# Delta rule of twelve heads on one Trainium2 core: inverse in 64x64 blocks, products by row halves, last norm by token

## The reference

```python
def rwkv7_scan(r, w, k, v, kk, a):
    def step(state, inp):
        r_t, w_t, k_t, v_t, kk_t, a_t = inp
        sa = jnp.einsum('bhvk,bhk->bhv', state, -kk_t)
        state = (state * w_t[:, :, None, :]
                 + sa[..., None] * (kk_t * a_t)[:, :, None, :]
                 + v_t[..., None] * k_t[:, :, None, :])
        return state, jnp.einsum('bhvk,bhk->bhv', state, r_t)
...
def rwkv7_mix(p, mu, w0, w_up, a0, a_up, g_up, kk_scale, k_a, r_k, lnx_g, lnx_b):
...
    y = rwkv7_scan(r_h, w_h, k_h, v_h, kk, a_h)
    mean = jnp.mean(y, axis=-1, keepdims=True)
    var = jnp.mean(jnp.square(y - mean), axis=-1, keepdims=True)
    y = ((y - mean) * lax.rsqrt(var + LNX_EPS)).reshape(b, s, RWKV_W) * lnx_g + lnx_b
    bonus = jnp.sum(r_h * k_h * r_k, axis=-1, keepdims=True) * v_h
    y = (y + bonus.reshape(b, s, RWKV_W)) * g
...
def memory_attention(q, mem, mem_norm_g, w_kv, q_gain, k_gain):
    k, v = jnp.split(rms_norm(mem, mem_norm_g) @ w_kv, 2, axis=-1)
    k = rms_norm(split_heads(k), k_gain)
    v = split_heads(v)
    q = rms_norm(q, q_gain)
    logits = jnp.einsum('bshd,bmhd->bhsm', q, k).astype(jnp.float32) / math.sqrt(HEAD_DIM)
    probs = jax.nn.softmax(logits, axis=-1)
    return jnp.einsum('bhsm,bmhd->bshd', probs.astype(v.dtype), v)
```

## Time and profile before

| what | value |
|---|---|
| median of 3 runs | 3707.04 us (3703.96 to 3710.41) |
| the profiled execution | 3713.19 us, span 3711.4 us |
| mean granted TensorE clock | 0.982 |
| PE busy, whole span | 3537.4 us (95%) |
| DVE / ACT / POOL busy | 1809.6 / 1230.9 / 482.6 us |
| chain that ended last, by engine | PE 84%, DVE 8%, ACT 1% |
| the same by line | PE acc L474 63%, L2197 2%, L2209 1%, L2213 1%, L2179 1%; DVE square_sums L2499 1% |

### The profile page before, as it was taken

One profiled execution on the slowest core, in us unless ns is written; L12 is line 12 of the kernel. 1 busy time (PEld: TensorE's weight loads), 2 busy tenths in 40 slices (PEclk: granted clock), 3 DMA queues, 4 the chain that ended last, 5 costly groups with the idle time before them and its releaser, 6 DMA issues.

```text
span 3711.4 us, 41381 instructions
## 1 busy us (share of the span) xinstructions
PE 3537.4 (95%) x16828; PEld 2753.0 (74%) x16828; DVE 1809.6 (49%) x2532; ACT 1230.9 (33%) x1911; POOL 482.6 (13%) x338
## 2 busy tenths in 40 slices
PE   3999999899999999999989999999999999999999
PEld 2765677675677778887788887788877887678887
DVE  6943336653435754336755555443446334554433
ACT  2433342333333432224333324222334223433221
POOL 1000001100001311002242321110100101011100
PEclk9999999899999999999989999999999999989999
DMA  4531122221112232223200001323322223112222
GB/s 189 182 119 52 51 74 76 80 89 52 57 46 86 80 108 95 93 88 125 72 7 1 1 24 46 117 91 97 91 91 80 95 92 97 40 35 95 93 97 85
DMA packets 83469, 295.91 MB, mean 80 GB/s; under 512 B 9424, under 2 KB 12624, under 8 KB 81232
## 3 DMA queue, kind: packets, MB, share of 16 engines
q1 hardware_dynamic: 82704, 289.06, 23.8%
q10 hardware_dynamic: 576, 4.19, 0.3%
HBM read 284.56 MB, written 8.65 MB: 79 GB/s over the span
## 4 chain that ended last, share of the span: by engine, by line
PE 84%; DVE 8%; issue 1%; ACT 1%; POOL 1%; DMA 0%; SPq 0%; DVEq 0%; ACTq 0%; POOLq 0%
PE acc L474 63%; PE aux L1511 2%; PE acc L1428 2%; PE acc L2197 2%; PE acc L2209 1%; PE aux L2179 1%; PE acc L1534 1%; PE acc L2213 1%; DVE w_lo L385 1%; PE aux L1413 1%; DVE square_sums L2620 1%; PE aux L2905 1%; DVE square_sums L2499 1%; DVE rstd L689 1%; PE aux L2910 0%
## 5 line engine op out<-in xcount | busy, mean ns | idle before, releaser
L474 PE MATMUL acc<-op_hi,w_hi 128*128 128x512 f32 x2624 | 1108.8, 423 | 48.9 <-DVE op_lo L1079 22.0
L474 PE MATMUL acc<-op_lo,w_hi 128*128 128x512 f32 x2624 | 1044.6, 398 | 0.0
L474 PE MATMUL acc<-op_hi,w_lo 128*128 128x512 f32 x2624 | 1044.1, 398 | 0.0
L378 ACT ACTIVATE w_hi<-raw 128x1024 fp32r<-128x1024 f32 (+2 forms) x476 | 494.3, 1039 | 1512.6 <-PE acc L474 1511.7
L385 DVE TENSOR_TENSOR w_lo<-raw,w_hi 128x1024 fp32r<-128x1024 f32 (+2 forms) x476 | 576.7, 1212 | 240.6 <-ACT w_hi L378 240.3
L474 PEld LDWEIGHTS acc<-op_hi,w_hi 128*128 128x128 f32 x2624 | 498.5, 190 | 216.6 <-issue 78.1
L474 PEld LDWEIGHTS acc<-op_hi,w_lo 128*128 128x128 f32 x2624 | 498.2, 190 | 119.9
L474 PEld LDWEIGHTS acc<-op_lo,w_hi 128*128 128x128 f32 x2624 | 500.0, 191 | 110.9 <-issue 11.7
L474 PE MATMUL acc<-ffn_hi,w_hi 128*128 128x512 f32 x800 | 317.0, 396 | 0.0
L474 PE MATMUL acc<-ffn_hi,w_lo 128*128 128x512 f32 x800 | 316.6, 396 | 0.0
L474 PE MATMUL acc<-ffn_lo,w_hi 128*128 128x512 f32 x800 | 316.5, 396 | 0.0
(11 more groups left out here) (485 smaller groups left out, 4413.6 us busy)
## 6 DMA issues: line engine op xcount, KB each, us to landing
raw<-in_w SPq DMA_DIRECT2D x436, 512.0 KB, 3.5
late_ada<-in_ada SPq DMA_DIRECT2D x32, 512.0 KB, 4.4
raw<-in_w SPq DMA_DIRECT2D x32, 384.0 KB, 3.1
x<-in_x SPq DMA_DIRECT2D x2, 2048.0 KB, 10.7
ada<-in_ada SPq DMA_DIRECT2D x4, 1024.0 KB, 23.1
ada<-in_ada ACTq DMA_DIRECT2D x4, 1024.0 KB, 16.6
x_mid<-x SPq DMA_DIRECT2D x16, 256.0 KB, 2.9
x<-x_mid SPq DMA_DIRECT2D x2, 2048.0 KB, 7.7
```

Source lines behind the costliest of these rows:

```text
L378: act.activation(self.w_hi[g % 2][:, 0:k, :], self.raw[s][:, 0:k, :], ACT.Copy).then_inc(self.split_hi.handle, 1)
L474: mm = pe.matmul(self.bank(s, g), w[:, k, :], a[:, k, 0:s.n], start=(k == 0 and q == 0), stop=(k == k_tiles - 1 and q == 2))
```

## The change

- The level masks become two stacked 64x64 blocks; those for level 6 go. A, D, C and G hold only the two 64x64 blocks on each diagonal, packed side by side (128x256 for a head instead of 128x512), and the block below the diagonal of A is kept apart (`below`).
- Levels 1 to 5 multiply 64x64 blocks: for each chunk the upper block sits in rows and columns 0 to 63 of the array and the lower in 64 to 127. Level 6 only has one block to fill: `below` times X, then D times that, copied into X. A level runs as F, S of head 0, then F, S of head 1.
- A product takes both heads: head 0's channels are rows 0 to 63 of the array and head 1's rows 64 to 127, each with a bank of its own. Five products of eight matmuls replace ten of four. The factor copies with zeroed halves on ScalarE go; the factors have two buffers. A's result is taken by four predicated copies of 64x256 and two plain ones.
- The turns come after the products, after the next pair's front has started.
- The last norm computes its variance as two columns for each chunk (one value for each token and head), takes root and reciprocal of 128x8 values, and spreads them over the channels with eight matmuls.
- `MemAttention` normalises keys and queries in one group with one reciprocal, and runs eight units for two heads each instead of sixteen.
- LEVEL 9.6 becomes 7.2, PAIR 60 becomes 48, and the planned pause 118 + 5 PAIR becomes 108 + 5 PAIR; the planned times of the parts are written anew.

```diff
-    for level in range(7):
+    for level in range(6):
         b = 1 << level
         m = (row // (2 * b) == col // (2 * b)) & (row % (2 * b) >= b) & (col % (2 * b) < b)
-        parts[f"level{level}"] = m
+        parts[f"level{level}"] = (m[:HD, :HD].astype(float)[None] * np.ones((2, 1, 1))).reshape(P, HD)
...
-    LEVELS, LEVEL, PAIR = 6, 9.6, 60.0
+    LEVELS, LEVEL, PAIR = 6, 7.2, 48.0
...
-        self.tA = [self.in_at[0] + 12.0] + [t + 1.0 for t in self.tB[:-1]]
-        self.t1 = [self.tA[0] + 28.0] + [t + 27.0 for t in self.tB[:-1]]
-        self.tC = [t + 2.0 for t in self.tB[1:]] + [self.tB[-1] + 57.0]
-        self.tL = [t + 33.0 for t in self.tC]
+        self.tA = [self.in_at[0] + 12.0, b0 + 1.0] + [t - 37.0 for t in self.tB[2:]]
+        self.tP = [t + 26.0 for t in self.tA]
+        self.t1 = [max(p + 17.5, a + 3.0) for p, a in zip(self.tP, self.tA[1:])] + [self.tP[-1] + 17.5]
+        self.tC = [t + 1.0 for t in self.tB[1:]] + [self.tB[-1] + 44.0]
+        self.tL = [t + 31.0 for t in self.tC]
...
         def products(m):
+            for i, (_, lhsT, rhs, _) in enumerate(self.products(m)):
+                yield self.product_time(m, i)
...
+                else:
+                    pe.wait_ge(*self.kept.ge(10 * m + 2 * i))
+                for n in range(NT):
+                    for e, rows in enumerate((slice(0, HD), slice(HD, P))):
+                        mm = pe.matmul(chunk((f1, f0)[e], n), chunk(lhsT[rows, :], n), chunk(rhs[rows, :], n),
+                                       start=True, stop=True)
+                mm.then_inc(*self.product.inc())
...
-            for i, (_, lhsT, rhs, _) in enumerate(self.products(m)):
-                yield self.t1[m] + 8.0 + 2.1 * i
...
-                for n in range(NT):
-                    mm = pe.matmul(chunk((f1, f0)[i % 2], n), chunk(lhsT, n), chunk(rhs, n), start=True, stop=True)
-                mm.then_inc(*self.product.inc())
...
                     for n in range(NT):
-                        mm = pe.matmul(chunk(self.first_banks[e], n), chunk(C[e], n), chunk(X[e], n),
-                                       start=True, stop=True)
+                        for i in range(2):
+                            mm = pe.matmul(block(self.first_banks[e], n, i), block(C[e], n, i), diagonal(X[e], n, i),
+                                           start=True, stop=True)
                     mm.then_inc(*self.first.inc())
-                for e in range(2):
-                    yield at + 4.0 + 2.0 * e
+                    yield self.level_time(m, level, e) + 2.2
                     pe.wait_ge(*self.copied.ge(self.level_count(m, level, e)))
...
                     for n in range(NT):
-                        mm = pe.matmul(self.packed(bank, level, 0, n), chunk(D[e], n),
-                                       self.columns_of(chunk(G[e], n), level, 1), start=True, stop=True)
...
+                        for i in range(2):
+                            mm = pe.matmul(self.packed(bank, level, 0, rows[i], n), block(D[e], n, i),
+                                           self.columns_of(block(G[e], n, i), level, 1), start=True, stop=True)
+                    for n in range(NT):
+                        for i in range(2):
+                            mm = pe.matmul(self.packed(bank, level, 1, rows[i], n), block(G[e], n, i),
+                                           self.columns_of(block(D[e], n, i), level, 0), start=True, stop=True)
                     mm.then_inc(*self.second.inc())
...
-            pe.matmul(y[:, :], core.c("blkmean"), self.ln_square, start=True, stop=True).then_inc(*self.varied.inc())
+            for n in range(NT):
+                mm = pe.matmul(y[:, 2 * n:2 * n + 2], chunk(self.ln_square, n), core.c("window")[:, 4:6],
+                               start=True, stop=True)
+            mm.then_inc(*self.varied.inc())
+            yield self.tL[m] + 8.5
+            pe.wait_ge(*self.inverted.ge(m + 1))
+            for n in range(NT):
+                for e in range(2):
+                    mm = pe.matmul(chunk(y[e * HD:(e + 1) * HD, :], n),
+                                   column(self.ln_factor[:, 2 * n + e:2 * n + e + 1], HD), core.c("ident"),
+                                   start=True, stop=True)
+            mm.then_inc(*self.spread.inc())
...
-                    dve.tensor_tensor(x, x, self.packed(bank, level, 0), ALU.add)
...
+                    for i, rows in enumerate((slice(0, HD), slice(HD, P))):
+                        x = self.diagonals_of(X[e], i).rearrange("p n (k c) -> p n k c", c=2 * b)[:, :, :, b:2 * b]
+                        grown = self.packed(bank, level, 0, rows).rearrange("p (n k) b -> p n k b", n=NT)
+                        dve.tensor_tensor(x, x, grown, ALU.add)
+                    d = self.columns_of(D[e], level, 0)
+                    dve.tensor_tensor(d, d, self.packed(bank, level, 1), ALU.add).then_inc(*self.updated.inc())
```

More of the change, by code:

```diff
@@ new lines, in __init__ @@
+        self.turn_v = Turns(core, "mem_v", [[v[:, j, t * P:(t + 1) * P] for j in range(2)] for t in range(MEM // P)],
+                            banks[0:2], lambda dve, t, bank: dve.tensor_copy(v_tok[:, t, :], bank[:, 0:2 * P]))
+        half = [slice(e * HD, (e + 1) * HD) for e in range(2)]
+        units = [{"keys": MEM,
+                  "scores": [(q(j)[half[e], t * P:(t + 1) * P], k[half[e], j, :]) for e in range(2)],
+                  "values": [[v_tok[:, b, (2 * j + e) * HD:(2 * j + e + 1) * HD] for b in range(MEM // P)]
+                             for e in range(2)],
+                  "out": o_tok[:, t, j * P:(j + 1) * P], "ready": []} for j in range(2) for t in range(NT)]
```

295 lines of the change are left out of this document (161 added, 134 removed).

## The result

| | before | after |
|---|---|---|
| median of 5 runs, us | 3709.54 | 3687.18 |
| lowest to highest, us | 3703.96 to 3710.41 | 3675.30 to 3695.75 |
| profiled execution, us (span) | 3713.19 (3711.4) | 3695.75 (3693.5) |

The ratio is 0.9944, with an interval of 0.9921 to 0.9968: faster, by 22 us where 50 were forecast. The range of 3611 to 3700 holds the time. The runs of the changed kernel lie 20 us apart, those of before 6 (in a later round of twelve runs 16, from 3700.45 to 3716.16). They go with the mean granted clock: 3695.75 and 3693.41 at 0.968, 3687.18 at 0.969, 3686.14 at 0.971, 3675.30 at 0.973. The profiled execution is the slowest of the five, so what its windows show of the low clock lies at the upper end.

A forecast was written before the change was run, and what follows sets the result against it. TensorE bounds the stage; 43.7 work, 10.5 waits and 5.1 clock loss make a 59.3 us period. Four periods minus 22, first pair 7, head 3, tail 18: 50 off the profiled 3713, 3657 against the median, range 3611 to 3700.

The forecast's parts named there:

- three signs of being wrong: Twos over 0.085 us, clock low in a third of the stage, or VectorE's queue putting over 6 us between products.
- TensorE's work, 43.7: Steady period: TensorE's work at full clock falls from 58.4 to 43.7 us, with the inverse giving minus 13.7.
- the first rival: Inverse and products: two array quarters do not run at once, 0.110 us for two instead of 0.055; 3730, chance 0.10.
- filling the pipe: Inverse of a steady period: 1.5 us for filling the pipe after 24 group starts, within a sum of 16.5.
- changes between full array and part of it: Steady period: some 9 more borders between full and partial array, 0.17 idle at one, plus 1.5 us.
- The waits, 10.5: Steady period: new TensorE waits of 3 us for F, copy, S, 6 between products, 1.5 for updates.
- The third rival: Delta rule stage: the chain of small steps is longer, waits 14 instead of 10.5, period 62.8; 3678, chance 0.20.
- Three stretches like the one of 1969 to 1981 instead of one: Steady period: the clock falls in three stretches like today's one of 1.7 us lost, costing 5.1 us.
- The second rival: Delta rule stage: clock at 1.2 GHz for half of each period's work, 21.9 us lost instead of 5.1; 3759, chance 0.13.
- The sixth pair and tail, minus 18: Sixth pair to next projection, 102.6 us: inverse minus 14, end minus 6, colder clock plus 2.
- First pair, minus 7: First pair, 56.3 us now: 29 of work, waits, and all 9.4 of today's clock loss kept, sum 49.4.
- Head, minus 3: Projection segment: the first pair's products and turns lose 5.4 us of TensorE work; minus 3 taken, between 0 and 5.4.

The follow-up runs named there:

- the period of 55.32: One steady period of the changed kernel with unread matmuls in TensorE's steady-period waits and the memory attention of before; that kernel measured 3656.03.
- the fillings: Changed kernel plus matmuls that nobody reads where TensorE waits: 3661.16 in the steady periods alone, 3654.63 with the first and sixth pair too.
- the later norm: Last norm's three VectorE operations behind X's copies, on the changed kernel with unread matmuls in steady periods, first and sixth pair: 3646.44, ratio 0.9835.

## Why the prediction was wrong

The way was right, but the gain was 22 us where 50 were forecast. TensorE's work and the sum of the waits came out as forecast; the clock term, 5.1 us in a period, and the clock in the sixth pair did not. Two of the prediction's own three signs of being wrong came true: the clock was low in two fifths of the stage (by the windows above 0.20 of 405 us are lost, and a stretch at 1.2 GHz loses half; a third was the sign), and 6.7 us of waits stood between the products (6 was the sign). That the time lies in the range is in part luck: the first pair gave 5.9 us more than forecast, while the four periods fell 19.6 short and the sixth pair 20.2.

**TensorE's work, 43.7: right.** In the fifth pair's period TensorE is busy 52.38; with 0.15 of 62.80 us lost it is 43.0 at full clock or more (some of the loss may fall in waits), and in the period of 55.32 at a clock of 1.00 it is 52.72 less 34 filling records at 0.24, 44.5. By pieces: a product of 16 records takes 1.09 from start to start, 0.136 for two (0.135 forecast). F of 16 records and S of 32, from start to start, on the timeline of the changed kernel (L2244 and L2248 are S):

```profile
2053.08 0.68 PE L2232 MATMUL acc<-squares,opB 64*64 64x64 f32 x16
2053.70 0.49 PE L2313 MATMUL aux<-square_sums,kk 128*128 128x128 f32 x2
...
2057.87 0.65 PE L2244 MATMUL acc<-opB 64*64 64x32 f32 x16
2058.35 0.63 PE L2248 MATMUL acc<-opB 64*64 64x32 f32 x16
2058.82 0.66 PE L2232 MATMUL acc<-squares,opB 64*64 64x64 f32 x16
```

F takes 0.62 and S 0.48 + 0.47, where 0.5 and 0.9 were the signs to look for: a two (two such records on opposite quarters) costs 0.078 in F and 0.06 in S, over the 0.055 taken and under the 0.085 from which the first rival decides. Ten F, ten S and four groups of level 6 at 0.6 make 18.1, where 16.5 were forecast with 1.5 for "filling the pipe"; no run shows that term by itself, nor the 1.5 for changes between full array and part of it.

**The first rival, no pairing: false.** Level 6 has eight records without a partner (L2261 above, 0.68) and takes as long as the sixteen of F, so the partner costs nothing. Both halves of F write one bank, in different partitions. The Trainium skill, page TensorEngine Tiling (Array Packing), section Restrictions and Gotchas, says that different row tiles cannot access the same PSUM bank at the same time; the trace does not agree: sixteen such records take 0.68, the time of eight.

**The waits, 10.5: right in sum, in part by luck.** F, copy, S 2.0 for 3; the products 3.4 + 1.8 + 1.5 = 6.7 for 6, the longest of them behind the norm's three operations as forecast. The updates were to cost 1.5 and left no wait; the 1.8 that stand in their place are the sequence's own (L2317 waits for its correction, L2550). At full clock the period is 55.3, with these places filled, where 43.7 + 10.5 = 54.2 was forecast. The third rival, a longer chain, did not come; that its 3678 lies near the measured time is chance.

**"Three stretches like the one of 1969 to 1981 instead of one, 5.1 us": this is the step that failed.** Against the periods at full clock with the fillings in the waits (54.3 for the second pair, 55.3 for the others) the four lost 10.1, 7.5, 11.6 and 7.5 us to the low clock, 36.6 together and 9.2 on average. That is 16.2 over four times 5.1. With the 3.4 by which the four at full clock are longer than four times 54.2, it makes up the 19.6 us by which the four periods are longer than forecast (256.8 and 237.2). The mistake was to price each stretch by the gap of before, after which the clock came back within 12 us. Behind the new gaps it stays at 1.2 GHz through some 10 us while TensorE is shown busy 10.00 of 10.00 at 0.54, and it falls a second time in the period. That the thinner work is what keeps it low is not shown: the stretch holds full-array products too, and before, ten such us at 0.50 stood in the first pair on the full array. The second rival named the stay at 1.2 GHz, its sign (a clock under 0.80) came in two of the four periods, 0.75 and 0.76, and its price of 13.4 us lost in a period was neared by the period of 66.92. The rival was put at a half of all work or nothing, and the middle was not priced.

**The sixth pair and tail, minus 18: wrong for the same reason in the inverse, and by some 5 us behind it.** It took 104.8 for 84.6. Up to the sequence's first product, at 2211.80, it took 64.0 for 47 and the 2 of "colder clock", 15 more. The clock was 0.72 in it, and 0.28 of 62.65, 17.5 us, is what that can cost at most, since what is low while TensorE idles costs nothing. From there to the projection it took 40.8 where 102.6 - 61 - 6 = 35.6 were forecast; before it took 41.3, and 37.0 with the norm alone, at 0.99. In the changed kernel the clock is 0.90 there, and TensorE waits 2.5 us for ScalarE ahead of the last variance (L2331) and 1.5 in the attention (L3010). How the 5 us divide is not settled. With the fillings, which brought the clock to 0.95, the sixth pair took 95.75, with some 8 us of their own in it (28 records more than in the changed kernel, each some 0.28), partly in waits that stood there anyway. The gaps of before did go: with the norm alone it is 93.6.

**First pair, minus 7: it was 12.9.** The clock's loss was kept at 9.4 and is 0.20 of 43.36, 8.7. The work is 35.98 - 8.7 = 27.3 for 29, and the waits are 7.4 for 11: the second pair's products cost 1.7 for 5 and ScalarE's copies 1.4 for 3, VectorE's updates 4.1 for 3. **Head, minus 3:** 2.8.

**What the parts are worth.** The norm alone is the whole of the measured gain. Products by row halves are about nothing. The inverse in blocks shortens TensorE's work by about what was forecast, and about one half of that is paid back in waits, the other to the clock; only with the clock held does a gain appear: 61.3 with the norm alone, 54.6 with everything, the fillings and the later norm. The inverse in blocks was not run without the products by halves.

## What to carry to other kernels

When a change thins out TensorE's work, cost its period twice, at the granted clock of now and with the clock low from the first new gap on through the work behind it, and let the likeliest value lie between. Before a large restructuring, test its smallest part alone: here a reciprocal of 8 columns in place of 512 gave as much as everything together. Where TensorE must wait, matmuls that nobody reads can be worth more than the wait itself; the granted clock of the windows tells where they pay, and in the first pair they did not.

## What the runs showed of the hardware that was not expected

- Two 64x64 blocks on opposite quarters of the array write one PSUM bank, in different partitions, in the time of one: 16 records are shown at 0.68 us, 8 unpaired ones at 0.68 too.
- The granted clock can stay at 0.50 to 0.72 while TensorE is shown busy almost without a pause: 10.00 of 10 us at 0.54, 59.97 of 62.65 at 0.72 in the sixth pair. The Trainium skill, page TensorE: Matmul & The Clock Gate, section HAM oscillation — how this bites in real kernels, puts such losses down to gaps in which the engine idles. The fall in the products agrees (3.37 us idle there). The sixth pair, with 2.7 us of idle time in all, and the fall at 2099 above, behind waits of at most 0.54 us, are not told by gaps alone.
- Some 35 added records in a period, 5 %, made it 5 to 9 us shorter.
- One kernel ran the same 783 records in 55.3 and in 58.5 us, period by period, so a time within one execution is not settled by its instructions alone.
